# A hybrid trunk step with a background expert loop: the weighted row sums that VectorE made are made on TensorE

## What is computed

```
act = gelu(einsum('thkd,td->thk', u[eb], xb))
y   = einsum('thk,thkd->td', gb * act, v[eb])
```

## Time and profile before

| | |
|---|---|
| median of 3 runs | 4865.04 us (4859.65 to 4870.78) |
| the profiled execution | 4873.52 us, its span 4871.7 us |
| rows with the sum on DVE / on PE | 632 / 648 |
| busy: PE, DVE, ACT, POOL | 2955.8, 3295.2, 1431.1, 1666.1 us |
| moved by DMA | 1556 MB, mean 319 GB/s |
| mean granted TensorE clock | 0.79 of full |

### The profile page before, as it was taken

One profiled execution on the slowest core, in us unless ns is written; L12 is line 12 of the kernel. 1 busy time (PEld: TensorE's weight loads), 2 busy tenths in 40 slices (PEclk: granted clock), 3 DMA queues, 4 the chain that ended last, 5 costly groups with the idle time before them and its releaser, 6 DMA issues.

```text
span 4871.7 us, 32513 instructions
## 1 busy us (share of the span) xinstructions
PE 2955.8 (61%) x8591; PEld 1464.7 (30%) x8591; DVE 3295.2 (68%) x6134; ACT 1431.1 (29%) x4023; POOL 1666.1 (34%) x1284
## 2 busy tenths in 40 slices
PE   7552968744565765545564555655878376666665
PEld 1341434432232320222422333233544232222222
DVE  0217657637788876777687786887961788766766
ACT  0111244301222331253132432324851133233222
POOL 0002322103452436444244343443420134555553
PEclk9766979976787888766887668876778699888888
DMA  6245966527995999999899799997962399999998
GB/s 236 97 147 206 354 260 229 212 99 307 381 420 233 374 356 405 397 379 408 359 371 401 302 385 377 361 410 289 332 253 82 127 381 387 415 422 422 415 422 364
DMA packets 227302, 1556.22 MB, mean 319 GB/s; under 512 B 31268, under 2 KB 34536, under 8 KB 54856
## 3 DMA queue, kind: packets, MB, share of 16 engines
q0 software_dynamic: 184320, 1342.26, 68.5%
q1 hardware_dynamic: 42824, 212.15, 11.4%
HBM read 1551.07 MB, written 3.24 MB: 319 GB/s over the span
## 4 chain that ended last, share of the span: by engine, by line
DMA 35%; DVE 26%; PE 21%; issue 7%; ACT 4%; POOL 4%; DVEq 1%; SPq 1%; PEldq 0%; ACTq 0%; PEld 0%; POOLq 0%
DMA core_ring<-in_l_uv,core_experts 24%; DVE core_ring L1418 5%; PE sum_rows L1453 4%; POOL core_ring L1410 4%; DVE core_yv L1427 4%; PE s_in_ps L425 2%; PE s1b_query_pq L1216 2%; DMA mod_w<-in_l_w_mod 1%; PE mod_ps L309 1%; DVEq L153 1%; PE s0b_out_po L490 1%; PE s1b_out_po L490 1%; PE p_query_pq L1216 1%; ACT L1439 1%; PE p_out_po L490 1%
## 5 line engine op out<-in xcount | busy, mean ns | idle before, releaser
L1410 POOL DMA_INDIRECT core_ring<-in_l_uv,core_experts x1280 | 1665.9, 1301 | 3170.9 <-DVE core_yv L1427 1094.9
L1418 DVE CUSTOM_DVE_ANT_0 core_ring<-core_ring,core_hc 128x1024 f32<-128x1024 f32 x1280 | 1549.2, 1222 | 648.1 <-DMA core_ring<-in_l_uv,core_experts 493.0
L1453 PE MATMUL sum_rows<-core_ring,core_diag 128*128 128x512 f32 x2592 | 1488.2, 720 | 778.8 <-ACT core_diag L1445 622.2
L1453 PEld LDWEIGHTS sum_rows<-core_ring,core_diag 128*128 128x128 f32 x2592 | 546.3, 225 | 1619.2 <-ACT core_diag L1445 1006.5
L1439 ACT ACTIVATE core_wt<-core_wt 128x1 f32<-128x1 f32 x1280 | 257.4, 201 | 1950.1 <-DVE core_wt L1418 1856.4
L1427 DVE SCALAR_TENSOR_TENSOR core_yv<-core_ring,core_wt,core_yv 128x1024 f32<-128x1024 f32 x632 | 809.3, 1281 | 24.2 <-ACT core_wt L1442 21.9
L1442 ACT ACTIVATE core_wt<-core_wt,core_gates 128x1 f32<-128x1 f32 x1280 | 376.8, 294 | 73.1
L1445 ACT ACTIVATE core_diag<-core_ident,core_wt 128x128 f32<-128x128 f32 x648 | 260.2, 402 | 21.2
L309 PE MATMUL mod_ps<-mod_w,mod_silu 128*2 128x512 f32 x384 | 192.5, 661 | 96.9 <-DMA mod_w<-in_l_w_mod 96.8
L1439 ACT ACT_TABLE_LOAD x110 | 141.1, 1283 | 72.3 <-DVEq L153 50.4
L1482 PE MATMUL sum_rows<-core_zero 128*128 128x128 f32 x160 | 37.6, 430 | 138.8 <-SPq L163 72.3
(11 more groups left out here) (592 smaller groups left out, 3153.5 us busy)
## 6 DMA issues: line engine op xcount, KB each, us to landing
mod_w<-in_l_w_mod SPq DMA_DIRECT2D x24, 2048.0 KB, 8.5
core_ring<-in_l_uv,core_experts POOLq DMA_INDIRECT x1280, 11.7
p_query_w<-in_l_peer_wq SPq DMA_DIRECT2D x32, 512.0 KB, 12.2
p_in_w<-in_l_w_in SPq DMA_DIRECT2D x5, 1664.0 KB, 6.8
s_in_w<-in_l_w_in SPq DMA_DIRECT2D x5, 1664.0 KB, 10.5
p_out_w<-in_l_w_out SPq DMA_DIRECT2D x2, 4096.0 KB, 14.8
s0a_query_w<-in_l_peer_wq SPq DMA_DIRECT2D x16, 512.0 KB, 4.6
s0b_query_w<-in_l_peer_wq SPq DMA_DIRECT2D x16, 512.0 KB, 7.9
```

The source lines that it names most:

```text
L1410: nc.gpsimd.indirect_dma_start(self.ring[:, r, :], None, core.a[f"l{layer}_uv"], bass.IndirectOffsetOnAxis(ap=self.experts[:, t, n:n + 1], ...
L1418: nc.vector.tensor_tensor_reduce(self.ring[:, r, 0:D], self.ring[:, r, 0:D], self.hc[:], 1.0, 0.0, ALU.mult, ALU.add, self.wt[:, r:r + 1]) ...
L1453: mm = nc.tensor.matmul(self.py[:, c * 512:(c + 1) * 512], self.diag[:, r, :], self.ring[:, r, D + c * 512:D + (c + 1) * 512], start=False ...
```

## The change

All 8 ring places go to PE, in every stage's triple and in the loop. Rates and leads stay as they are. DVE makes no `add_row` any more; its `yv` is still cleared and still added at a tile's end.

```diff
-    LOOP_PLACES = places_on_pe(5)
+    LOOP_PLACES = places_on_pe(8)
...
-PROMPT_RATES = {"norm": (7.0, PE_4, 5), "in": (3.0, PE_2, 4), "qk": (7.5, PE_4, 5), "attend": (2.0, PE_2, 0), "out": (6.0, PE_2, 4),
-                "query": (1.3, PE_0, 2), "select": (1.7, PE_8, 3)}
-MIXER_RATES = {"norm": (2.0, PE_4, 5), "in": (1.6, PE_0, 4), "decay": (4.0, PE_4, 3), "gla": (1.6, PE_8, 4), "pool": (2.0, PE_2, 4),
-               "out": (2.0, PE_0, 4), "query": (0.8, PE_0, 2), "select": (1.5, PE_8, 3)}
-LATENT_RATES = {"norm": (6.0, PE_4, 5), "in": (3.0, PE_0, 4), "qk": (5.5, PE_4, 5), "attend": (1.6, PE_2, 0), "out": (5.5, PE_0, 4),
-                "query": (3.0, PE_0, 2), "first select": (1.4, PE_8, 3), "select": (1.8, PE_8, 3)}
+PROMPT_RATES = {"norm": (7.0, PE_8, 5), "in": (3.0, PE_8, 4), "qk": (7.5, PE_8, 5), "attend": (2.0, PE_8, 0), "out": (6.0, PE_8, 4),
+                "query": (1.3, PE_8, 2), "select": (1.7, PE_8, 3)}
+MIXER_RATES = {"norm": (2.0, PE_8, 5), "in": (1.6, PE_8, 4), "decay": (4.0, PE_8, 3), "gla": (1.6, PE_8, 4), "pool": (2.0, PE_8, 4),
+               "out": (2.0, PE_8, 4), "query": (0.8, PE_8, 2), "select": (1.5, PE_8, 3)}
+LATENT_RATES = {"norm": (6.0, PE_8, 5), "in": (3.0, PE_8, 4), "qk": (5.5, PE_8, 5), "attend": (1.6, PE_8, 0), "out": (5.5, PE_8, 4),
+                "query": (3.0, PE_8, 2), "first select": (1.4, PE_8, 3), "select": (1.8, PE_8, 3)}
...
-        modulation_stage(core, 1, "mod1", (4.0, PE_0, 3))
+        modulation_stage(core, 1, "mod1", (4.0, PE_8, 3))
```

## The result

The changed kernel takes 5000.69 us (median of 4 runs, 4993.79 to 5007.83) against 4867.91 us before (4 runs): ratio 1.0272, 95% interval 1.0246 to 1.0298. It is 133 us slower; 5035 was predicted, 170 us slower, with a range of 4945 to 5120.

The account below looks back on a forecast made before the run. The prediction took no single engine to bound the kernel, each stage having its own limit. Its stage terms summed to +170 us on the profiled 4873.5, giving 5043.5, less 8.5 for the median: 5035 us, range 4945 to 5120.

Parts of the forecast that it names:

- A: Whole kernel: PE paces the projections and queries, and DVE's relief is not on the path; +170 us, chance 0.88.
- points 1 to 3: Moved rows lengthen PE's work: s_in +56 us, s0b query +31, s1a in +12, s1b in +22.
- The price of 1.76 us: Any stage: PE's time at full clock for one row, four 512-column records, with others ahead of it.
- Point 4: s0b out, 37 rows: 126 us against 109.8, +16; DVE's 47 us less worth nothing, since PE ends later.
- Point 6: mod, 51 rows: rows between matmuls delay weight loads a little, +8 us; prompt in and the two queries +1.
- Point 8: qk stages, 38 rows, called DVE-bound: DVE's relief, mostly taken back by PE's bursts, gives -11 us together.
- Point 9: Norms, decay and pool: DVE's relief against PE's longer bursts at a low clock; 0, bounds -30 and +50 us.
- Point 7: s1b attend, 57 rows: a head takes 5.8 us instead of 5.28, +25 us; the other two attend stages 0.
- B: Whole kernel: DVE's adds pace the stages, so the change is faster; -68 us, 4797 us, chance 0.05.
- C: Whole kernel comes out even: PE's extra 121 us given back by relief in other stages; about 4865 us, chance 0.03.
- D: Loop becomes PE-bound at the half clock level: +300 us on top of A, 5335 us, chance 0.04.
- at most 600: Whole kernel: with the clock at full everywhere, at most some 600 us of PE's busy time could come back.

Follow-up runs that it names:

- e1: Kernel before, adds still on DVE, plus two 512-column matmuls of zeros on PE for each of its 632 rows: 5049.97 us, ratio 1.0356.
- e4: Kernel before with the row sums on PE only in the projections and queries: 4983.08 us, ratio 1.0223.
- e6: Kernel before; loop with all 8 places on PE and two zero matmuls after each row sum; projections with 4 of 8 places on PE: 5198.23 us.
- e2: Kernel before with the 632 adds on DVE left out, DVE only freeing the ring places: 4813.23 us, ratio 0.9873.
- e5: Changed kernel and kernel before, each with the 54 rows of the two latent qk stages gathered at half size: 4971.35 and 4849.95 us.
- e3: Kernel before with the row sums on PE only in norms, decay, modulation and the loop: 4859.50 us, ratio 0.9968.
- e8: Kernel of e3 with 4 of 8 places on PE in the attend stages: 4848.41 us, ratio 0.9941.
- e9: Kernel of e8 with 4 of 8 places on PE in s0b out, and out-stage row sums only behind the tile's second half of matmuls: 4876.53 us, ratio 1.0002.

## Why the prediction was right

By its own steps, the difference predicted and that of the windows:

| | predicted | in the trace |
|---|---|---|
| 1 `s_in` | +56 | +50.4 |
| 2 `s0b` query | +31 | +29.6 |
| 3 `s1a` in, `s1b` in | +12, +22 | +7.8, +19.9 |
| 4 `s0b` out | +16 | +5.5 |
| 5 small out stages | +10 | +11.5 |
| 6 mod; small projection and queries | +8; +1 | -5.7; -0.5 |
| 7 `s1b` attend; the other two | +25; 0 | +9.3; +8.2 |
| 8 qk, three stages | -11 | +4.6 |
| 9 norms, decay, pool | 0 | -12.7, -5.7, +1.9 |
| 10 loop; gla | 0; 0 | +1.5; +6.6 |

The rows of this table add up to +132 us; all other stages together have -8. The mechanism, A, was right: e1 gives the loss of points 1 to 3 with matmuls that wait for nothing, e4 with those stages alone. The price of 1.76 us was right too: e6's doubled loop keeps PE busy 1.75 us for each of its 304 x 2, and in `s_in` PE's busy time grows by 59.9 us for 35 rows (140 records), 1.71 each. The stage pays 50.4, not 56: PE wasn't quite full, and its idle time there falls from 14.4 to 4.9 us.

The signs that the prediction asked for came: the query at 176.8 us and 350 GB/s (178 and 350), the layer 1 projections at 93.7 and 106.0 (98 and 108), the loop at 770.6 (770), a row sum's record at 619 ns (below 720), the clock at 0.90 (0.85 or more). Only gla, which was to stay, has +6.6.

The sum was 37 us too high, in these terms:

- Point 4 valued DVE's relief in `s0b` out at nothing, "since PE ends later". e1 against the change says it is worth 23 us there (+28.2 and +5.5), e2 says 14. Before the change PE stood still twice for 14.6 us, until ACT, which weighs rows in order behind DVE's dots, came to the next tile's transposed rows:

```profile
1181.15 1.97 PE L477 MATMUL s0b_out_pt<-core_ident,core_h 128*128 128x128 f32 x8 [14.55 <-ACT s0b_out_rT L502]
...
1212.01 15.43 PE L490 MATMUL s0b_out_po<-s0b_out_w,s0b_out_rT 128*128 128x512 f32 x32 [14.56 <-ACT s0b_out_rT L502]
```

  With the adds left out (e2) these waits are 9.8 us each: shorter DVE batches shorten them. In the changed kernel they are gone, and PE works without a gap from 1193.69 on, 15.0 us into the stage. So PE does end last, as the prediction said; its 126 us were too long by about the 8 for transposes and their waits and the 2 at the end.
- Point 6 had mod's sign wrong. It is not the clock: with a clock of 0.94 and the adds kept, e1 gains 1.6 us of 204, as much as e4, e6 and the half-row run of the kernel before, which don't touch the stage (1.0 to 2.1); with the adds out at a clock of 0.79, e2 gains 5.9; the change 5.7. What helps is that the adds leave DVE; through which wait is not shown.
- Point 8 expected 11 us from relief in qk. e2 and e5 show the relief turned into a wait for rows: the gathers were the limit, and a buffer that PE frees late makes it worse (for qk this second part is argued, see e5). That is the wait that took the place of the one removed. The prediction named PE's bursts as what takes the relief back, but not the gathers behind them, and called the stages DVE-bound.
- Point 9 gained 16.5 us, within its bounds, and 6.6 of them went to gla, whose own constants met the gathers (e3).
- Point 7 was right in kind for `s1b` attend: PE paces it at 248 of 262.7 us, 5.17 us a head where 5.5 was estimated. PE's own part is 3.1 us a head at a clock of 0.96 (248.2 less 224 added records at 0.44) and not 3.4, and a head takes 5.5 us instead of 5.8, so +9.3 instead of +25. The other two attend stages were put at nothing and have +5.2 and +3.0, and e1 has +6.3 and +1.9 with the adds kept, so that is PE's time too. That the sum over all three is only 8 us off is luck.

So 170 came within 37 us partly by luck: the terms that were too high (points 1 to 4, 6, 7 and 9, some 63 us) are set off in part by those that were too low (25, of which qk 16 and gla 7).

Smaller slips of the working changed little. The first matmul of `s1a` in starts 11.1 us into the stage (at 2573.88), not 12. The 26 us above the DMA's floor in qk are `s1a`'s alone; `s1b`'s 85.8 us at 331 GB/s add 18. DVE's busy time fell to 2546 and not 2486 us, since records of adds overlap those beside them.

Rivals: B falls with e2 (60 us, not 180). C falls with the result. D falls with the loop's clock of 0.99; e6 shows that it would be real at twice the load. On the clock the Trainium skill ("TensorE: Matmul & The Clock Gate", section "Why this matters for your kernels") says that idle gaps between bursts of matmuls put the clock back to its lower level. The trace agrees in direction: with the gaps filled the granted clock goes from 0.64 to 0.77 in `s1a` qk, from 0.85 to 0.99 in the loop and from 0.79 to 0.90 over all. Some 300 us of PE's busy time came back with it (1112 less 811), of the at most 600 that the prediction gave. It paid little, because the stages with low clocks were not held by PE.

## What to carry to other kernels

Ask of each stage, not of the kernel, whether the engine that takes the work has room: the same row sum was free in a DMA-bound stage (4 of 8 places in `s1a` in), 1.4 to 1.6 us where PE was full, and the fullest engine of the whole kernel was worth 60 us when 744 us of its busy time vanished. Where three engines are near level, split the work to level them (e8) rather than move it all. And a slot of a ring that is freed by an engine with other things queued ahead is freed late, and the consumer then waits for data (e9: 3.2 us of waits for rows became 34.0).

## What the runs showed of the hardware

POOL's gather instruction went from 1301 to 1096 ns in the mean when the adds left DVE (1665.9 to 1402.8 us in all). The adds read two SBUF tensors on DVE, and the Trainium skill, "SBUF — State Buffer", section "SBUF: two separate sides", has such an operation and a GpSimd one that reads SBUF shut each other out. But with the adds left out and PE as before (e2) the mean is still 1300 ns, with both (e1) 1280. So it isn't the adds by themselves; it is the dots, which stay and read two tensors as well. Two lines of the kernel before, from its loop:

```profile
4420.93 1.23 DVE L1418 CUSTOM_DVE_ANT_0 core_ring<-core_ring,core_hc 128x1024 f32<-128x1024 f32 x1
4421.15 1.82 POOL L1410 DMA_INDIRECT core_ring<-in_l_uv,core_experts  x1 [3.16 <-DVE core_yv L1427]
```

The gather instruction begins during a dot, takes 1.82 us where the median is 0.94, and ends 0.81 us after the dot's end. Counted out of the whole trace, 548 of the 552 gather instructions over 1.1 us end 0.79 to 0.84 us after a dot, an add or another DVE instruction with two tensors (495 of them after a dot), and so do 332 of 334 in the changed kernel and 661 of 665 in e2. So the trace agrees with the rule. What shortens the mean is when POOL starts: 688 gather instructions begin during a dot in the kernel before and 808 in e2, where DVE frees places and goes on to its next dot, but 410 in the changed kernel, where PE frees them (mean 1.40 to 1.52 us each, the others 0.95 to 1.05). No stage is seen to gain or lose by it.
